# Two causal attentions of one layer: two blocks made one, heads outermost, exponentials normalised on GpSimd, outputs by features

## The reference

```python
def causal_softmax_attention(q, k, v, scale):      # latent attention, v of 64 per head
    for start in range(0, S, 128):
        s = einsum(q[start:end], k[:end]) * scale
        s = where(s_idx <= t_idx, s, -inf)
        p = softmax(s, axis=-1)
        outs.append(p @ v[:end])

def stick_breaking_attention(q, k, v):
    z = einsum(q, k) * scale                       # before = s_idx < t_idx
    log_not = where(before, log_sigmoid(-z), 0)
    between = cumsum(log_not, reverse) - log_not
    a = where(before, exp(log_sigmoid(z) + between), 0)
    return a @ v
```

## Time and profile before

| | |
|---|---|
| median of 3 runs | 4098.18 us (4091.08 to 4105.27) |
| the profiled execution, its own time | 4099.14 us |
| its span in the trace | 4097.1 us |
| granted TensorE clock, mean | 0.989 of full speed |
| PE busy | 3961.6 us, 97% |
| PEld / DVE / ACT / POOL busy | 84% / 62% / 38% / 14% |
| PE's share of the chain that ended last, L3603 alone | 11% |

### The profile page before, as it was taken

The page is one execution under the profiler, slowest core; times in us unless marked ns, Lnnn a source line. Parts: engine busy times, 40 slices in busy tenths (PEclk is TensorE's granted clock), DMA queues, the critical chain, the costliest instruction groups (busy, mean ns, idle before and its releaser), DMA issues. The chain is left out here.

```text
span 4097.1 us, 50314 instructions
## 1 busy us (share of the span) xinstructions
PE 3961.6 (97%) x20625; PEld 3450.7 (84%) x20625; DVE 2543.1 (62%) x3750; ACT 1538.7 (38%) x2114; POOL 593.2 (14%) x425
## 2 busy tenths in 40 slices
PE   8999998999999999999999999999999999999998
PEld 7778897789999999999997887688888887678887
DVE  6432677689888875777776533775444442875443
ACT  3221225323666663333333224543222232743322
POOL 1000201200223332344322100100001110001000
PEclk9999999999999999999999999999999999999999
DMA  3344005325688899898873444142233434242322
GB/s 131 109 138 158 22 33 186 114 103 175 221 292 317 294 329 334 332 348 339 340 303 126 141 131 124 63 146 93 94 101 108 129 128 135 74 144 98 103 93 82
DMA packets 269056, 689.72 MB, mean 168 GB/s; under 512 B 19187, under 2 KB 52339, under 8 KB 251932
## 3 DMA queue, kind: packets, MB, share of 16 engines
q1 hardware_dynamic: 222748, 527.11, 37.5%
q0 software_dynamic: 36864, 134.23, 9.5%
q10 hardware_dynamic: 9216, 25.17, 1.5%
HBM read 585.50 MB, written 100.96 MB: 168 GB/s over the span
## 5 line engine op out<-in xcount | busy, mean ns | idle before, releaser
L1273 ACT CAST pe_w_high<-pe_w_raw 128x2048 fp32r<-128x2048 f32 (+1 forms) x168 | 316.3, 1883 | 529.8 <-DMA pe_w_raw<-in_peer_v_units 245.9
L1365 DVE TENSOR_TENSOR pe_w_low<-pe_w_raw,pe_w_high 128x2048 fp32r<-128x2048 f32 (+1 forms) x168 | 382.1, 2274 | 178.3 <-ACT pe_w_high L1273 176.6
L1160 PE MATMUL ps<-xn_p_high,pe_w_high 128*128 128x384 f32 (+1 forms) x1088 | 382.7, 352 | 31.5 <-DVE pe_w_low L1365 18.1
L2266 ACT CAST tail_w_high<-tail_w_raw 128x2048 fp32r<-128x2048 f32 (+3 forms) x124 | 221.4, 1790 | 443.0 <-DMA tail_w_raw<-in_w_in 144.0
L2275 DVE TENSOR_TENSOR tail_w_low<-tail_w_raw,tail_w_high 128x2048 fp32r<-128x2048 f32 (+3 forms) x124 | 266.5, 2153 | 185.0 <-ACT tail_w_high L2266 184.7
L1160 PE MATMUL ps<-xn_p_high,pe_w_low 128*128 128x384 f32 (+1 forms) x1088 | 373.1, 343 | 0.0
L1160 PE MATMUL ps<-xn_p_low,pe_w_high 128*128 128x384 f32 (+1 forms) x1088 | 372.9, 343 | 0.0
L1190 PE MATMUL ps<-pe_far_hidden_high,pe_w_high 128*128 128x384 f32 x1024 | 345.9, 338 | 14.7 <-DVE pe_near_hl L1491 11.6
L1190 PE MATMUL ps<-pe_near_hl,pe_w_high 128*128 128x384 f32 x1024 | 344.1, 336 | 0.0
L1190 PE MATMUL ps<-pe_far_hidden_high,pe_w_low 128*128 128x384 f32 x1024 | 344.0, 336 | 0.0
L1578 POOL DMA_INDIRECT home_pe_row<-in_peer_u,pe_expert x128 | 177.8, 1389 | 572.9 <-DVE pe_act L1551 377.0
(11 more groups left out here) (651 smaller groups left out, 9385.0 us busy)
## 6 DMA issues: line engine op xcount, KB each, us to landing
pe_w_raw<-in_peer_u_units SPq DMA_DIRECT2D x64, 1024.0 KB
pe_w_raw<-in_peer_v_units SPq DMA_DIRECT2D x64, 1024.0 KB
in_w_raw<-in_w_in SPq DMA_DIRECT2D x34, 1024.0 KB, 5.5
tail_w_raw<-in_w_up SPq DMA_DIRECT2D x32, 1024.0 KB, 5.5
tail_w_raw<-in_w_down SPq DMA_DIRECT2D x32, 1024.0 KB, 5.1
pe_w_raw<-in_w_in SPq DMA_DIRECT2D x28, 1024.0 KB
tail_w_raw<-in_w_in SPq DMA_DIRECT2D x28, 1024.0 KB, 5.0
dram_peer_hidden<-pe_rings_r ACTq DMA_DIRECT2D x64, 384.0 KB
```

Of the source, the lines that this page charges most:

```text
L1160: last = pe.matmul(ps[:, q, 0:n], w[:, s, at], xp[:, 4 * i + c, 0:n], start=(i == 0 and c == 0 and p == 0), stop=(i == 1 and c == 3 and p ...
L1273: act.copy(ring.flat(hi, u), ring.flat(raw, u)).then_inc(w_hi, 1)
L1365: dve.tensor_tensor(ring.flat(lo, u), ring.flat(raw, u), ring.flat(hi, u).bitcast(F32), ALU.subtract).then_inc(w_lo, 1)
L2266: act.copy(hi, raw).then_inc(self.w_hi, 1)
```

## The change

The two blocks become one, `two_attentions`; `Turn`, `load_early`, `latent_attention` and `stick_breaking` go.

- The latent units are ordered by heads: `units = [(h, m) ...]`, m = 0 to 3 innermost.
- POOL multiplies the exponentials in place by the reciprocals (`normalised`, 32 operations per layer of 128 x 128 to 128 x 512), between the exponential and the transposes. The transposes of unit j now wait for it, and stand three units behind the scores instead of two (`TURNED`). The reciprocal of unit i - 1 follows the maxima of unit i on DVE.
- The two clears of `sb_q` stand in POOL's list behind units 3 and 7.
- The values of a head are multiplied once per head (`latent_outputs`), when its four units are turned: four matmuls of 512, 384, 256 and 128 columns, with the values of a pair of heads as stationary operand, so the output comes by features. 80 matmuls of 64 columns per layer become 32.
- The 16 transposes of the turn and the 32 evictions to `y` go. In their place, per head: one rounding of 64 x 512 on ACT (`leading`) and one remainder of 64 x 512 on DVE (`remainder`), at the second unit two heads on.
- The rotation's due times are 10.0 and 3.9 apart (before 15.0 and 4.6).
- The end of the latent part and the start of stick-breaking are interleaved by hand: the score set of head 0, the last turn, one `occupy`, the last outputs, score sets 1 and 2, four `occupy` (before: four in all). DVE does `keep` of heads 0 and 1, then `softplus(0)`, then the last remainder.
- SP loads retention's inputs after the last latent outputs instead of after the turn.

The arithmetic is otherwise the same. The diff, cut:

```diff
+    units = [(h, m) for h in range(MH) for m in range(NT)]
+    N = len(units)
+    TURNED, SUMMED = 3, 4
+    AT = [5.2 * (i // NT) + (0.0, 0.9, 2.1, 3.5)[i % NT] for i in range(N + SUMMED + 1)]
+    ROTATE = 10.0, 3.9
+    half = lambda h: slice(M_V * (h % 2), M_V * (h % 2) + M_V)
...
+        @block.tensor
+        def _(pe):
...
+            def turn(j):
+                m = units[j][1]
+                pe.wait_ge(n_done, j + 1)
+                if j >= 2:
+                    pe.wait_ge(t_read, j - 1)
+                for c in range(m + 1):
+                    last = pe.transpose(ps[:, 3 + j % 2, c * P:(c + 1) * P], logit[:, j % 3, c * P:(c + 1) * P], k.ident[:, :])
+                last.then_inc(t_done, 1)
+
+            def latent_outputs(h):
+                pe.wait_ge(t_read, NT * (h + 1))
+                if h >= 2:
+                    pe.wait_ge(ya_lo, h - 1)
+                pair = slice(P * (h // 2), P * (h // 2) + P)
+                for c in range(NT):
+                    last = pe.matmul(ps[:, 5 + h % 2, c * P:T], heads.v[:, c, pair],
+                                     pT[h % 2][:, 4 * c:3 * c + NT, :].rearrange("p m q -> p (m q)"),
+                                     start=(c == 0), stop=(c == NT - 1))
+                last.then_inc(pv_done, 1)
...
+            for i in range(N + 2):
+                if i < N:
+                    latent_scores(i)
+                if i >= TURNED:
+                    turn(i - TURNED)
+                if i >= SUMMED and (i - SUMMED) % NT == NT - 1:
+                    latent_outputs((i - SUMMED) // NT)
...
+            whole(0)
+            turn(N - 1)
+            occupy(1)
+            latent_outputs(MH - 1)
+            whole(1)
+            whole(2)
+            occupy(4)
...
+        @block.vector
+        def _(dve):
...
+            def remainder(h):
+                dve.wait_ge(ya_hi, h + 1)
+                dve.tensor_tensor(ya_low[half(h), h // 2, :], ps[half(h), 5 + h % 2, :], ya_high[half(h), h // 2, :].bitcast(F32),
+                                  ALU.subtract).then_inc(ya_lo, 1)
+
+            def attention():
+                for i in range(N + 2):
+                    yield AT[i] + 0.5
+                    if i < N:
+                        dve.wait_ge(s_done, i + 1)
+                        dve.tensor_reduce(nmx[:, i:i + 1], ps[:, i % 3, 0:(units[i][1] + 1) * P], AX.X, ALU.max,
+                                          negate=True).then_inc(max_done, 1)
+                    if 1 <= i <= N:
+                        dve.wait_ge(p_done, i)
+                        dve.reciprocal(rl[:, i - 1:i], ls[:, i - 1:i]).then_inc(r_done, 1)
+                    if i >= 2 * NT and i % NT == 1:
+                        yield AT[i] + 0.6
+                        remainder(i // NT - 2)
...
+            weave(attention(), rotation.combine(dve, *ROTATE))
+            keep(0)
+            keep(1)
+            dve.wait_ge(pv_done, MH)
+            softplus(0)
+            remainder(MH - 1)
+            keep(2)
...
+        @block.gpsimd
+        def _(pool):
+            def normalised(i):
+                cols = slice(0, (units[i][1] + 1) * P)
+                pool.wait_ge(r_done, i + 1)
+                pool.tensor_scalar(logit[:, i % 3, cols], logit[:, i % 3, cols], rl[:, i:i + 1], None, ALU.mult).then_inc(n_done, 1)
+
+            suffix.prepare(pool)
+            for i in range(N):
+                normalised(i)
+                if i in (NT - 1, 2 * NT - 1):
...
+                    pool.memset(empty[n], 0.0).then_inc(suffix.prepared, 1)
+                    pool.wait_ge(suffix.prepared, n + 2)
...
+        @block.scalar
+        def _(act):
...
+            for i in range(N + TURNED):
+                if i < N:
+                    cols = slice(0, (units[i][1] + 1) * P)
+                    act.wait_ge(max_done, i + 1)
+                    if i >= 3:
+                        act.wait_ge(t_done, i - 2)
+                    act.activation(logit[:, i % 3, cols], ps[:, i % 3, cols], ACT.Exp, bias=nmx[:, i:i + 1],
+                                   accum_out=ls[:, i:i + 1]).then_inc(p_done, 1)
+                if i >= TURNED:
+                    kept(i - TURNED)
+                if i >= 2 * NT and i % NT == 1:
+                    leading(i // NT - 2)
```

More of the change, by code:

```diff
@@ L112 @@
 UC, OUTS = 4, 4
[L115 to L139, removed]
 def delta_rule(k, name, at, small, qT, kT, k_tok, v_tok, tables, out_norm, coming, z_dram, z_raw, ent):
@@ L1662, in sines @@
             act.activation(dst[:, :], src, ACT.Sin).then_inc(self.done, 1)
[L1665 to L1679, removed]
 class SuffixTables:
@@ L1801, in stick_breaking, with two_attentions @@
-def stick_breaking(k, name, place, qT, kT, v, tables, lo, outT, early, turn):
+def two_attentions(k, l, place, heads, ya, loads, rotation, work, ent, suffix, empty, qT, kT, v, lo, yb, later):
     nc, ps = k.nc, k.ps
@@ new lines, in two_attentions @@
+    logit, pT, st = work
+    nmx, ls, rl = st[:, 0, :], st[:, 1, :], st[:, 2, :]
+    ya_high, ya_low = ya
+    y_high, y_low = yb
+    sem = lambda n: k.sem(f"mla{l}_{n}")
+    s_done, max_done, p_done, r_done, n_done, t_done, t_read, pv_done, ya_hi, ya_lo = (
+        sem("s_done"), sem("max_done"), sem("p_done"), sem("r_done"), sem("n_done"), sem("t_done"), sem("t_read"),
+        sem("pv_done"), sem("y_hi"), sem("y_lo"))
+    landed, landed_later = sem("early"), sem("later")
+    sem = lambda n: k.sem(f"sb{l}_{n}")
@@ new lines, in two_attentions @@
+    sb = place
+    z, u, w = sb("z", [P, 3, W]), sb("u", [P, 2, W]), sb("w", [P, 2, W])
+    hi = sb("hi", [P, 2, W], F32R)
+    z_done, z_kept, ln_done, sp_done, sums, args, expd, o_done, o_kept, chain = (
+        sem("z_done"), sem("z_kept"), sem("ln_done"), sem("sp_done"), sem("sums"), sem("args"),
+        sem("exp"), sem("o_done"), sem("o_kept"), sem("chain"))
+    act_chain, y_hi, y_lo = sem("act_chain"), sem("y_hi"), sem("y_lo")
+    yT = sb("yT", [P, 4, T])
+    units = [(h, m) for h in range(MH) for m in range(NT)]
```

414 lines of the change are left out of this document (160 added, 254 removed).

## The result

| | before | after |
|---|---|---|
| median | 4097.88 us (4091.08 to 4105.27, 6 runs) | 4122.78 us (4118.49 to 4130.14, 6 runs) |
| ratio | | 1.0060, 95% interval 1.0046 to 1.0073 |
| span of the profiled execution | 4097.1 us | 4123.9 us |

The changed kernel is 0.6% slower, 25 us. The forecast was 4145 with a range from 4112 to 4162: the sign and the range hold, but the forecast loss was 47 us, nearly twice what came. It came nearest to the first rival (4127), in which the chain binds and the clock stays.

What follows compares the result with a forecast made beforehand. The latent block was taken as bound by PE's own work, after the change by a cross-engine chain. Terms 11.2 + 1.7 + 1.3 + 9.2 = 23.4 us per layer, 46.8 for two, gave 4145 us, range 4112 to 4162.

Steps and rivals of the forecast that it cites:

- first rival: Latent part: the chain binds but PE's clock stays at full, 2 x 14.2 = 28.4 us, 4127; chance 0.16.
- PE's own work is not what decides: Latent heads: PE's own work 6.1 us per head against about 5.8 before; on PE alone about even.
- The chain of 8.7 us through DVE's wait in `remainder`: Latent heads: maxima of unit 2 wait behind DVE's remainder for ACT; 8.7 us per head, PE waiting 2.6.
- The term of +11.2 per layer: Latent part: the chain starts stick-breaking's score set 0 at 63.1 us after the block's start, before at 51.9.
- First outputs at 8.0: Latent start: first outputs at about 8.0 us, from 6.5 of PE's work and some 1.5 for table load and first exponentials.
- upper bound of 1.27: GpSimd's multiplication, 128 x 512: taken as a copy's 0.62 us, at most a two-operand operation's 1.27, costing 0.65 per layer.
- a sign of being wrong: Trace after: GpSimd operations over 1.3 us with transposes waiting for them would prove the forecast wrong.
- third rival: GpSimd counts: 0.65 + 2.6 us more per layer, partly from slower rotation pieces; 4152, up to 4162; chance 0.10.
- The clock, +9.2 per layer: Latent part: six PE waits of 2.6 us halve the clock, 0.9 x 6 x 1.7 us per layer.
- The end, +1.7: Latent end to first suffix sums: PE's fixed list takes 15.5 us, before 13.8, per layer.
- The rotation's load, +1.3: First `ret_swap` on DVE moves to 2518 but its load lands at 2519.5; the chain moves with it, +1.3 us.
- The sum: Per layer 11.2 + 1.7 + 1.3 + 9.2 = 23.4 us, for two layers 46.8.

Runs made afterwards that it cites:

- fill run: Five useless matmul calls on PE ahead of the outputs of heads 1 to 6, against the changed kernel without GpSimd's multiplications: 4142.4 us, ratio 1.0104.
- the run with three fills: Three useless matmul calls on PE ahead of each head's outputs, against the changed kernel without GpSimd's multiplications: 4121.53 us, ratio 1.0068.
- the two kernels with one long wait per head: Changed kernel without GpSimd's multiplications (4146.0 us), and changed kernel with the multiplication written with two full operands (4139.55 us).
- late remainder: Changed kernel with DVE's remainder two units later: 4106.30 us, ratio 1.0023; with two of the last four `occupy` also removed: 4106.50 us, ratio 1.0025.

## Why the prediction was nearly right, and where it failed

- **PE's own work is not what decides:** right; 5.66 us per head (fill run) against 6.1 worked out and 5.8 before.
- **The chain of 8.7 us through DVE's wait in `remainder`:** right, 8.48 to 8.87 in the trace, each link in its place, and moving that one operation gave 16.5 of 25 us back. The term of +11.2 per layer was too small: the first stick-breaking scores came 16.3 and 14.8 us later. Against the forecast start of the scores at 63.1, the first outputs are 1.57 late (9.57, forecast 8.0); of the remaining 3.5 and 1.9, some 2.8 and 1.6 are the two falls of the clock in the first layer and the one in the second, and about 0.5 in each is the distance from the first to the second outputs, with its wait for GpSimd.
- **First outputs at 8.0:** held only without GpSimd's work (7.84 measured there). GpSimd was costed at 0.62 us with an upper bound of 1.27 for 512 columns. It took 1.79 on average and 1.56 at the least, outside both ends, and the first head has nothing to hide it behind. The clears of `sb_q`, also costed at nothing, stand in front of PE's waits for GpSimd of 1.15 and 2.70 us at the first and the second outputs (1.15 and 2.22 in the second layer). In later heads the multiplication adds nothing to the chain, as the sum said (the heads are 8.48 and 8.87 apart with it and, in the run with three fills, without it), though it does hold PE for 0.72. The prediction had named GpSimd operations over 1.3 us with the transposes waiting for them as a sign of being wrong, and this sign came. Of its third rival, the slower rotation pieces did not come (0.66 to 0.69 us but for one of 0.97 and one of 0.77); the extra time showed on GpSimd's side. The Trainium skill (GPSIMD Engine Reference, Performance versus the Vector engine) has GpSimd at about half VectorE's rate with two inputs; the trace agrees for the two-operand form (1270 ns against some 0.67 us of VectorE's rotation pieces); the form with a scalar is slower still, 1788 ns.
- **The clock, +9.2 per layer: the step that failed.** "PE waits 2.6 in one piece, ahead of its outputs" does not hold in the changed kernel: the multiplication splits it into 0.72 and 2.00 (or 1.61). The clock fell two times in one layer and once in the other, where the sum had 0.9 x 6, so the term of 9.2 per layer measured some 2.8 and 1.6; and the one fall of the second layer stands behind GpSimd's wait of 2.22, not behind the chain's. With the multiplications away the piece was whole, the clock fell in all six, and the kernel took 4146.0. So for one long wait per head both the rate of falls and the price held (twelve falls cost 19.6 us in the traces, 1.6 each, forecast 1.7); what was wrong is the size of one wait, which came out of a duration on an engine that I had put down at no cost. An operation hidden under a wait still moves the wait's edges.
- **The end, +1.7:** the first suffix sums came 15.1 and 14.85 us behind the first scores, before 13.84; up to retention it is 0.3 and 0.6. The marker was ill chosen: what happens up to the first suffix sums is partly given back behind them.
- **The rotation's load, +1.3:** too large; it is one wait of 0.4 us. VectorE's waits in the first layer's latent part (us in total, times, longest), where the second row is the wait in `remainder`, once per head from head 2 on, and the last is the load (the first includes the time before the block starts):

```profile
DVE mla_st L1834 <- PE ps L1715: 41.0, 11, 23.3
DVE ya_low L1826 <- ACT ya_high L1917: 8.8, 6, 1.5
DVE mla_st L1838 <- ACT mla_logit L1937: 1.6, 3, 0.8
DVE ret_swap L1990 <- DMA ret_swap<-dram_pf: 0.4, 1, 0.4
```

- **The sum:** forecast 23.4 per layer to the suffix sums, measured 17.6 and 15.8. Of the 13.4 us too much in two layers, the clock accounts for nearly all; the rotation's load and the end were too large as well, and the first head's GpSimd work offsets some 3. The median moved by 24.9 where the forecast had 46.8, so 22 us were too much there. The other 8 or 9 lie outside this sum: 1.35 is given back between the suffix sums and retention, and most of the rest is where the blocks start and what lies between and behind them, which has the same instructions before and after. The third rival's 4152 would be 4151 when counted against the median, as the forecast was.
- **The Trainium skill** (TensorE: Matmul & The Clock Gate, Why this matters for your kernels) names only PE-idle gaps longer than nearly all of these. Here the trace disagrees: in the two kernels with one long wait per head the granted clock fell at 24 of 24 waits of 2.15 to 3.04 us. That rule would have forecast 4127 and been nearer in this case, but for the wrong reason.

## What to carry over

Follow the chain of one iteration across the engines, and put on an in-order engine's list nothing that waits for another engine ahead of what a third engine waits for: here one remainder, moved two units later, was worth two thirds of the loss. Before costing an operation at nothing because a wait hides it, ask how it divides that wait; a wait in two pieces may keep the clock where one piece loses it (ten waits with two falls here, against twelve of twelve), though two pieces of 1.23 and 1.12 us lost it as well. And measure up to a point behind which nothing is given back: filling matmuls at a seam can look like a loss of 1.5 us that the next wait would have cost anyway.

## What was not expected of the hardware

- On GpSimd a multiplication by a per-row scalar is the slowest way of those measured: 1788 ns on average for 128 x 512, against 1270 for the same product with the scalar spread as a second full operand, and about 616 for a copy. With no VectorE operation on two operands beside them the two forms take 1.56 and 1.04 us, with a rotation piece beside them mostly 1.92 and 1.41. For 128 columns it is 0.60 against 0.40, but for the two of 1.88 and 1.69.
- Making that operation faster made the kernel 17 us slower, leaving it out 23 us slower, and adding useless matmuls to the latter 24.5 us faster, mostly through the granted clock. In the traces, the first suffix sums of the two layers come 13.7 and 14.0 us later and 19.6 earlier, all told.
- Of the changed kernel's six waits of 2.00 or 2.01 us ahead of outputs, two were followed by half clock, of its four of 1.61 or 1.62 none. A wait of 2.70 us, in the same place in two kernels, was followed by half clock in one of them only, and one of 2.22 us in that place in the second layer was too. In that place, waits of 2.54 and 2.44 us (late remainder, with four and with two `occupy`) kept the clock, and without GpSimd's work 1.23 and 1.12 us, with a transpose between them, lost it. In the kernel before, the clock stayed at 1.00 behind an idle time of 3.15 us at 1823.85, just above the range in which the prediction counted. What tells these apart is open.
